# T2 of the fast matrix products made by GpSimd as a subtraction in SBUF, in place of an accumulating transfer from DRAM

## The reference

```
x = x + merged @ w_out[l]
h = rms_norm(x, norm_ffn[l])
x = x + (jax.nn.silu(h @ ffn_gate[l]) * (h @ ffn_up[l])) @ ffn_down[l]     # hidden width 5632
return rms_norm(x, norm_final)
```

## Time and profile before

| what | us |
|---|---|
| median of 3 runs (2754.2 to 2756.76) | 2756.17 |
| the profiled execution | 2760.97 |
| its span | 2759.2 |
| TensorE busy in it | 2709.7 |
| VectorE, ScalarE, GpSimd busy in it | 1832.2, 1233.6, 792.6 |
| mean granted TensorE clock | 0.995 |

### The profile page before, as it was taken

How to read it: one execution, slowest core, us unless ns; L and a number is a source line. 1 busy time by engine, 2 the same in 40 slices (tenths; PEclk the granted TensorE clock), 3 DMA queues, 4 the chain that set the end, 5 groups by cost and what they waited for, 6 DMA issues and landing times.

```text
span 2759.2 us, 38078 instructions
## 1 busy us (share of the span) xinstructions
PE 2709.7 (98%) x14050; PEld 2182.2 (79%) x14050; DVE 1832.2 (66%) x3007; ACT 1233.6 (45%) x2050; POOL 792.6 (29%) x751
## 2 busy tenths in 40 slices
PE   8999999999999999999999999999999999999998
PEld 7767777777777777888887888888888877888876
DVE  5657364363563654422268888888888889888886
ACT  5444343343333433322335555555455456555555
POOL 2324234233342342554440221122222222111112
PEclk9999999999999999999999999999999999999999
DMA  5222122222222223433435576667766678887783
GB/s 190 77 77 103 67 85 87 82 75 95 72 88 73 76 95 115 158 150 127 150 135 169 149 181 173 169 169 187 170 155 150 174 182 244 208 249 177 199 217 107
DMA packets 328920, 386.77 MB, mean 140 GB/s; under 512 B 142640, under 2 KB 229168, under 8 KB 315824
## 3 DMA queue, kind: packets, MB, share of 16 engines
q1 hardware_dynamic: 281808, 315.33, 35.4%
q0 software_dynamic: 38176, 53.76, 11.3%
q10 hardware_dynamic: 8768, 15.47, 1.6%
HBM read 333.10 MB, written 55.57 MB: 141 GB/s over the span
## 4 chain that ended last, share of the span: by engine, by line
PE 88%; DVE 6%; ACT 2%; issue 2%; DMA 1%; DVEq 1%; POOL 0%; SPq 0%; ACTq 0%; POOLq 0%
PE dense L2084 12%; PE dense L2086 11%; PE dense L2085 11%; PE work L2462 11%; PE work L2466 11%; PE work L2464 11%; PE dense L2462 3%; PE dense L2466 3%; PE dense L2464 3%; DVE ring_lo L1777 1%; PE work L2252 1%; DVEq L1330 1%; DMA tight<-w_down 1%; PE work L2304 1%; ACT whi L857 1%
## 5 line engine op out<-in xcount | busy, mean ns | idle before, releaser
L786 POOL TENSOR_TENSOR wlo<-raw,whi 128x512 fp32r<-128x512 f32 x400 | 541.5, 1384 | 891.1 <-ACT whi L857 891.1
L857 ACT ACTIVATE ring_hi<-wblock 128x512 fp32r<-128x512 f32 x840 | 527.8, 632 | 513.7 <-PE work L2466 337.0
L1777 DVE TENSOR_TENSOR ring_lo<-wblock,ring_hi 128x512 fp32r<-128x512 f32 x840 | 571.8, 686 | 121.7 <-ACT ring_hi L857 115.2
L2462 PE MATMUL work<-ring_hi,S_hi 128*128 128x512 f32 x1460 | 572.4, 392 | 10.9 <-DVE ring_lo L1777 10.8
L2464 PE MATMUL work<-ring_hi,S_lo 128*128 128x512 f32 x1460 | 569.1, 390 | 0.0
L2466 PE MATMUL work<-ring_lo,S_hi 128*128 128x512 f32 x1460 | 568.9, 390 | 0.0
L2084 PE MATMUL dense<-H_hi,whi 128*128 128x512 f32 x1208 | 505.3, 418 | 10.0 <-DVE H_lo L1358 8.5
L2086 PE MATMUL dense<-H_hi,wlo 128*128 128x512 f32 x1208 | 473.4, 392 | 0.0
L2085 PE MATMUL dense<-H_lo,whi 128*128 128x512 f32 x1208 | 473.3, 392 | 0.0
L857 ACT ACTIVATE whi<-raw 128x2048 fp32r<-128x2048 f32 (+1 forms) x109 | 198.2, 1821 | 469.7 <-PE dense L2086 386.7
L2462 PEld LDWEIGHTS work<-ring_hi,S_hi 128*128 128x128 f32 x1460 | 274.4, 188 | 79.2 <-DVE ring_lo L1777 14.8
(11 more groups left out here) (333 smaller groups left out, 3517.7 us busy)
## 6 DMA issues: line engine op xcount, KB each, us to landing
raw<-w_slots SPq DMA_DIRECT2D x101, 1024.0 KB, 4.8
wblock<-w_gu SPq DMA_DIRECT2D x88, 1024.0 KB, 9.0
wblock<-w_down SPq DMA_DIRECT2D x60, 512.0 KB, 6.7
wblock<-w_gu POOLq DMA_DIRECT2D x22, 1024.0 KB, 10.0
S_raw<-s_dram SPq DMA_DIRECT2D x14, 1024.0 KB, 8.5
tight<-w_down SPq DMA_DIRECT2D x20, 512.0 KB, 8.7
gates_dram<-gout ACTq DMA_DIRECT2D x32, 256.0 KB, 2.1
gin<-gates_dram SPq DMA_DIRECT2D x16, 512.0 KB, 3.6
```

The lines of the kernel that those rows point to most:

```text
L786: done = nc.gpsimd.tensor_tensor(wlo[s][:, at], raw[s][:, at], whi[s][:, at].bitcast(f32), SUB)
L857: return A.activation(dst, src, ACT.Copy, scale=scale)
L1777: V.tensor_tensor(ring_lo[w % RING][:], of_tile(j, source[product], k), ring_hi[w % RING][:].bitcast(f32), SUB).then_inc(ring_lo_ready, 1)
L2462: PE.matmul(banks[a][:], S_hi[product][:, k, tok], high[:], start=(k == 0 and product not in (3, 2)), stop=False, skip_group_check=True)
```

## The change

GpSimd makes T2 with one subtraction for each pair, block 22 less T1, both in SBUF, into block 12, as soon as `ring_low` has read T3 of that pair. `ring_high` of product 6 waits for the subtraction of its own pair, and SP's load of the next block 11 also for the step's last. The transfers of line 818 are gone. `block_pieces` and `block_dmas` stay, for the loads.

```
+T2_FIRST = 0
+def made(j, k):
+    return sum(depth(i) for i in range(T2_FIRST, j)) + k + 1

-        sums_ready, t2_added = sem("sums_ready"), [sem(f"t2_added{h}") for h in range(2)]
+        sums_ready, t2_made = sem("sums_ready"), sem("t2_made")
                                                      # SP, the loads of step j + 1
                 sp.wait_ge(ring_lo_ready, after(j, 5))
+                sp.wait_ge(t2_made, made(j, depth(j) - 1))
                 load_block(j + 1, 11)
                                                      # GpSimd, step j
-                for h in range(2):
-                    pool.wait_ge(ring_lo_ready, item_of(j, 7, min((h + 1) * HK // 2, depth(j)) - 1) + 1)
-                    for into, src in block_pieces(j, 11, h, 12):
-                        pool.dma_start(into, src, accum_op=ADD).then_inc(t2_added[h], 16)
+                for k in range(depth(j)):
+                    pool.wait_ge(ring_lo_ready, item_of(j, 7, k) + 1)
+                    cols = slice(k * P, (k + 1) * P)
+                    nc.gpsimd.tensor_tensor(blocks(j)[12][:, :, cols], blocks(j)[22][:, :, cols],
+                                            blocks(j)[11][:, :, cols], SUB).then_inc(t2_made, 1)
                                                      # ScalarE, ring_high
                 elif product == 6:
-                    act.wait_ge(t2_added[2 * k // HK], 16 * block_dmas(j, 11, 2 * k // HK))
+                    act.wait_ge(t2_made, made(j, k))
```

## The result

The changed kernel takes 2873.82 us in the median of three runs (2870.89 to 2877.72), against 2756.17: a ratio of 1.0426 [1.0412, 1.044]. The forecast was 2865 us, 3.9% more. The profiled execution of after has a span of 2872.0 us, 112.8 more than that of before, at the same mean clock of 0.995.

What follows compares the result with a forecast made beforehand. TensorE was taken to bound the kernel, fed by VectorE. Terms 77 + 8 + 16 + 7 + 4 - 3 = 109 us put the profiled 2760.97 at 2870, the median at 2865 us, 3.9% more; range of 8 in 10: 2815 to 2908.

Steps and rivals of the forecast that it cites:

- What bounds the kernel: TensorE is busy for 98% of the span, so a change counts only where it makes TensorE wait or ends a wait.
- What is removed: T2's transfers of line 818 go; two late ones in the 6-deep steps end TensorE waits, -3 us, and no others do.
- The size of the hold: Each GpSimd subtraction holds VectorE's next two-SBUF-operand instruction in product 7 by 1.02 us, taken from line 1558.
- Product 7: At depth 8, seven holds before `ring_low` of (7, 7) ends, 7.1 us, less cover of 1.8: TensorE 5.3 us late.
- The seam: Steps 1 to 10: eight holds make the stores of the sums 8.2 us late, TensorE at (6, 6) 7.7; 77 us together.
- Step 11 and the last two: Step 11, its seam in product 7 without cover, loses 8 us; steps 15 and 16, five holds each, lose 7 together.
- Step 0: TensorE at half its clock from 1472 us covers VectorE's holds; loss between 0 and 8 us, taken as 4.
- TensorE's waits: Sign in the profile after: TensorE's waits for `ring_low` near 115 us instead of 8.5, seven or so a step of about 0.8.
- The clock rival: TensorE's share of work in product 7 drops and its granted clock falls in each of 17 steps: 2892 us, chance 0.17.
- The longer hold (1.29): Each subtraction holds VectorE up to 1.29 us, or longer through the pieces of 128 columns: 2901 us, chance 0.06.
- The stream that keeps the port: VectorE's unbroken stream in product 7 isn't broken; subtractions fall into idle time of products 5 and 6: 2806 us, chance 0.10.
- Not slower: The hold of `ring_low` is absent or below 0.06 us, so only the 3 us gain remains: 2753 us, chance 0.05.

Runs made afterwards that it cites:

- the zeros: Changed kernel with GpSimd writing zeros to T2's tiles in place of the subtraction, same place and waits, no T2 computed: 2749.66 us, 0.9968 of the kernel before.
- The last two pairs alone: Changed kernel with the subtraction kept only for the last two pairs of each step, GpSimd writing zeros for the others: 2769.72 us, 1.0039 of the kernel before.
- the later copy: Changed kernel with ScalarE's copy into `u2buf` one item later, result whole: 2859.95 us, 1.0364 of the kernel before.
- the copy: Changed kernel with GpSimd copying block 22 into block 12 in place of subtracting, one SBUF input instead of two: 2787.13 us, 1.0098 of the kernel before.
- the other operands: Changed kernel with GpSimd subtracting two contiguous pieces of a constant tile, so the result isn't T2: 2872.67 us, 1.0414 of the kernel before.

## Why the prediction came out

- **What bounds the kernel: right.** A delay of VectorE in product 7 was a delay of TensorE. The 132 holds cost 0.94 us of span each, though TensorE is the busy engine in both profiles.
- **What is removed: mis-sized.** The term was -3 us and the zeros show -8.5 by the medians. "No other transfer ends TensorE's waits" was the step that failed. TensorE's waits are put to VectorE, and what VectorE and ScalarE had waited for was followed only for the tight transfer. The row of ScalarE's waits for S parts (11.7 us in 3, above) stood in the same view of before. About 4.4 us of it reached the end (steps 10, 12, 14), and the steps 15 and 16 gave 4.7 where 3 stood ("at most as much again" was 1.10 us as a wait of TensorE, but the steps got shorter by more than these two waits).
- **The size of the hold: mechanism right, size a little off.** 1.10 us on `ring_low`, against 1.02. The reference, line 1558, has 0.75 us alone and 1.77 held, and `hidden2`, of that same form, was held for 1.02 again. `ring_low` takes 0.68 alone, so the difference taken from line 1558 was 0.08 short for it. The long `S_lo` of step 0 (L1828) took 3.38 us where it took 2.28 in before: 1.10 too. The bound of 1.29 was GpSimd's own time, which was right as a length, and 0.2 of it overlap. The forecast named "one record in two of lines 1777 and 1808"; in effect it is one in two of the pair, but `ring_low` in all steps but step 0. `t_three` was under way when GpSimd started and wasn't stopped. All 132 subtractions held something. VectorE's busy time grew by 1.01 us for each and not by 1.10, since records that overlap count once, and more of them follow each other without a gap now.
- **Product 7: the number right, the count wrong.** 5.3 us forecast and 5.6 in step 13, the only step with nothing else in it; 5.6 in the steps 12 and 14 too, against zeros. But "seven holds lie before `ring_low` of (7, 7) ends" is one too many, and the cover of 1.8 us is that of (7, 7), while the last item that TensorE waits for is (7, 6). In after six holds of 1.10 make `ring_low` of (7, 6) 6.6 us late. In before it ends at 1710.51 and TensorE starts on it at 1711.71, so its cover is 1.2: 6.6 - 1.2 = 5.4, and 0.2 more stand in the restart after a wait (below). One hold too many and 0.6 us of cover too many nearly cancel, which is luck.
- **The seam: right in kind, 0.5 us high, and its cover mis-sized.** 7.7 forecast, 7.2 in five steps. The last two pairs alone and the later copy show its two parts. The cover of 0.5 us was worked out from step 3, where ScalarE waits 2.58 us for the stores, and from the mean of ten steps, 2.2. In the steps 5, 7 and 8 it waits 1.4, as here in step 5 (before, ScalarE's copy, VectorE's `ring_low` of (6, 6), TensorE's start on it):

```profile
1883.00 0.60 ACT L857 ACTIVATE u2buf<-dense 128x512 f32<-128x512 f32 x1 [1.40 <-DMA s_dram<-u2buf]
```

```profile
1884.15 0.69 DVE L1777 TENSOR_TENSOR ring_lo<-wblock,ring_hi 128x512 fp32r<-128x512 f32 x1 [1.82 <-ACT ring_hi L857]
```

```profile
1886.15 0.39 PE L2462 MATMUL work<-ring_hi,S_hi 128*128 128x512 f32 x1
```

`ring_low` ends at 1884.84, so the cover is 1.3 us. With it one account gives all the kernels whose step is set at (6, 6). In the mean of the steps 5, 7 and 8 the first store of the sums is later than in before by 8.3 us in after, 4.2 where VectorE makes T2, 2.8 with the copy and 1.9 with the last two pairs. Less 1.3, plus 0.3 for TensorE's restart (below), that is 7.3, 3.2, 1.8 and 0.9, and the steps lost 7.1, 3.0, 1.6 and 0.8. So the last two pairs lost 0.9 and not 1.7 because the cover is 0.8 us larger than taken. "ScalarE's wait for the stores in `u2buf` as long as now" contradicted the sum's own steps: if product 7 makes ScalarE's place in the ring 5.6 us late and the stores 8.3, the wait has to grow. It went from 2.2 us in the mean to 4.2.
- **Steps 1 and 4: not foreseen.** They lose 3.1 and 4.2 us more than their like. SyncE's timeline of after has the sixteen stores of `u2buf` (us to issue them) in step 3 and in step 4:

```profile
1754.31 7.82 SPq L704 DMA_DIRECT2D s_dram<-u2buf  x16
```

```profile
1837.70 9.67 SPq L704 DMA_DIRECT2D s_dram<-u2buf  x16
```

ScalarE's copy that waits for them, in step 4, and the stretches of 2 us around it (TensorE's busy time is the first number behind the length, the granted clock stands behind POOL):

```profile
1849.60 0.60 ACT L865 ACTIVATE u2buf<-work 128x512 f32<-128x512 f32 x1 [6.10 <-DMA s_dram<-u2buf]
```

```profile
1848.00:1850.00 2.00, 0.21 (x1) 0.00 (x0) 0.00 (x0) 0.40 (x1) 0.00 (x0) 1.00 0.50 85
...
1852.00:1854.00 2.00, 2.00 (x7) 1.58 (x7) 1.91 (x4) 1.14 (x3) 0.00 (x0) 0.65 0.40 67
1854.00:1856.00 2.00, 2.00 (x6) 1.52 (x6) 1.73 (x3) 0.26 (x1) 0.00 (x0) 0.50 0.40 67
```

From the first issue to the copy it is 11.9 us in step 4 (1837.70 to 1849.60) and 9.2 in step 3 (to 1763.49). TensorE stood 3.3 us, and then its clock was at 0.65 and 0.50 of full (0.50 is 1.2 GHz) in two stretches of 2 us. In before one step has such slow stores too: 9.46 us of issue in step 6, which was 0.6 us longer than its like. So the change took away the slack in which such a delay had gone nearly unseen. Why it comes in some steps wasn't settled. It isn't the issue alone: with the last two pairs, step 4 issues its sixteen in 8.13 us, and the copy still starts 12.2 us behind the first. That step lost 6.5 us.

- **Step 11 and the last two: right.** Step 11 is 7.6 us for 8, the steps 15 and 16 are 3.9 and 3.8 against zeros for 3.6 (four holds where the sum had five, and less cover, as in product 7 of the deep steps).
- **Step 0: 4 forecast, 7.6 measured.** The lower clock covered the holds less long than taken. TensorE is back at the full level from 1482 us, and the holds go on through `S_lo`, to 1487.6. And behind that wait it falls once more, where before had 1.00 (TensorE's row, then its busy time and granted clock):

```profile
1489.44 0.47 PE L2470 MATMUL work<-ring_hi,S_hi 128*128 128x512 f32 x1 [2.69 <-DVE ring_lo L1785]
```

```profile
1488.00:1490.00 2.00, 0.56 (x3) 1.00 0.00 0
...
1492.00:1494.00 2.00, 2.00 (x7) 0.50 0.34 131
```

The result was between the stated ends of 0 and 8.
- **The sum.** Against zeros the holds cost 124.6 us where the terms gave 112, and the removal gave 8.5 by the medians (11.8 by the spans) where 3 stood. The two errors, 13 us and 6 to 9, cancel in good part: some of the nearness of 2865 to 2873.8 is luck. The range of the likeliest case, 2845 to 2885, would have held either error alone.
- **TensorE's waits: 84.8 us where 115 were expected**, in 126 places. A step has six such waits in product 7 and not seven. And the loss for an item is 2.31 - 1.38 = 0.93 us, where the wait that the rows give is 0.65. The rest isn't idle in the records: the first matmul behind a wait has 0.34 us to the next start, not 0.23, and the last one ahead of it is recorded for its 0.39 and not the 0.23 that it takes in a stream. That is 0.11 + 0.16 = 0.27 us lost in restarting after each wait, 34 us in 126, and 84.8 + 34 = 119 is close to the 124.6 that the holds cost; the rest would be, as far as it goes, the slower clock in the steps 0, 1 and 4.

**The rivals.** The clock rival falls. TensorE works 2.76 of 4 us in product 7 and the granted clock stays at 1.00:

```profile
1732.00:1736.00 4.00, 2.76 (x11) 1.97 (x12) 4.00 (x5) 1.15 (x2) 2.75 (x2) 1.00 0.00 0
```

It had something in it, though, in the steps 0, 1 and 4, where a wait of about three microseconds stood ahead of a low clock. The longer hold (1.29) falls, by 1.10 in the rows and by the other operands. The stream that keeps the port falls: in the unbroken stream of product 7 each subtraction got in behind the instruction that was under way. Not slower falls with the result, and the zeros show what it would have taken: only without GpSimd's reads is the kernel at 2750 us.

The Trainium skill, "SBUF — State Buffer", section "Who interferes with whom", has a VectorE instruction with two SBUF inputs contend with a GpSimd instruction only if that one reads SBUF. The zeros, which read nothing, held no `ring_low`, and the transposes with one input weren't held: the trace agrees. The same page says that the pair of ports is an exclusive lock, held by whichever starts first for its whole instruction. The trace agrees here too, if GpSimd's 0.38 us are read as its own wait: the subtraction waits for `t_three`, and `ring_low` then waits for the subtraction. What VectorE loses is 0.2 us less than the instruction.

## What to carry to other kernels

Before work is moved to an idle engine, look whether the engine that it is meant to spare reads two operands from the same memory in an unbroken stream: here each GpSimd subtraction of 1.3 us held VectorE 1.1 us, more than the 0.6 us that the work costs VectorE itself, and an instruction that only writes cost nothing at the same place. Find the lead that the feeding engine has at each point of a step, since a delay at the start of a burst is paid at once and one at its end may be hidden. For what a removed transfer gives back, read the waits of every engine that feeds the bound one, not of the bound one alone. And take the cover of a step from several steps: here a single one had 1.2 us less than its like.

## What the runs showed of the hardware that I had not expected

- The lock works both ways within one item: GpSimd's record grows from 1.30 to 1.68 us (copy 0.62 to 1.02), VectorE's from 0.68 to 1.79 (copy 1.09). A held instruction ends 0.54 to 0.55 us behind GpSimd's end in the rows above.
- Zeros of 0.53 us hold nothing and aren't held. The same is so of a transpose (one input) beside a subtraction.
- A wait of TensorE costs 0.27 us beyond the idle time in the records.
- From the first of SyncE's sixteen small stores to the copy that waits for them it is 9.2 to 9.5 us in six of the steps 1 to 10 of after, 10.8 and 10.9 in two and 11.7 and 11.9 in two. With no slack behind them the long ones cost 3 to 6 us of a step, part of it the lower clock.
